# Other PSUM banks for the products of a fused qkv stage, and one place per chunk for its small products

## The reference, cut to what matters

```python
q = _heads(hx, w[:, :hd], na_q_g[j])          # product, then RMS norm over each head's 64 columns
k = _heads(hx, w[:, hd:2 * hd], na_k_g[j])
v = _heads(hx, w[:, 2 * hd:])
k_c = _heads(hc, w[:, hd:2 * hd], na_k_g[j])  # the same for 256 context tokens
v_c = _heads(hc, w[:, 2 * hd:])
x = x + gx1 * (_neighbourhood_attention(q, k, v, k_c, v_c, na_rpb[j]) @ na_w_out[j])
```

## Time and profile before

| | us |
|---|---|
| median of 3 runs | 1366.85 (1366.1 to 1367.48) |
| the profiled execution's own time | 1367.44 |
| its span in the trace | 1365.2 |
| TensorE busy in the span | 1330.2 |
| VectorE, ScalarE, GpSimd busy | 810.3, 594.2, 429.6 |

### The profile page before, as it was taken

The page is one execution under the profiler, slowest core; times in us unless marked ns, Lnnn a source line. Parts: engine busy times, 40 slices in busy tenths (PEclk is TensorE's granted clock), DMA queues, the critical chain, the costliest instruction groups (busy, mean ns, idle before and its releaser), DMA issues.

```text
span 1365.2 us, 20841 instructions
## 1 busy us (share of the span) xinstructions
PE 1330.2 (97%) x8320; PEld 1141.9 (84%) x8320; DVE 810.3 (59%) x1223; ACT 594.2 (44%) x952; POOL 429.6 (31%) x439
## 2 busy tenths in 40 slices
PE   6999999999999999989999999999899999999999
PEld 6888898899997788858878888887577777999999
DVE  6678576899776452386633444343667765855443
ACT  4336545566664132244421244222545544666432
POOL 3443221222420003244400044111466552388200
PEclk9999999999999999999999999999999999999999
DMA  6777457865556231344534444444523221555552
GB/s 256 261 252 270 139 175 275 296 204 184 181 172 207 69 96 59 97 166 156 168 127 156 150 139 146 142 144 159 181 93 108 94 93 32 188 184 185 184 185 78
DMA packets 63967, 220.13 MB, mean 161 GB/s; under 512 B 6912, under 2 KB 10240, under 8 KB 63872
## 3 DMA queue, kind: packets, MB, share of 16 engines
q1 hardware_dynamic: 63584, 218.56, 47.9%
q10 hardware_dynamic: 288, 0.25, 0.1%
HBM read 217.73 MB, written 1.05 MB: 160 GB/s over the span
## 4 chain that ended last, share of the span: by engine, by line
PE 89%; DVE 6%; issue 2%; POOL 1%; ACT 1%; DMA 1%; DVEq 0%; ACTq 0%; POOLq 0%
PE ps L508 26%; PE ps L522 25%; PE ps L520 25%; PE ps L563 2%; PE ps L882 1%; DVE wlo L1463 1%; PE ps L909 1%; PE ps L896 1%; PE ps L828 1%; DVE Alo L1886 1%; DVE tmp L1901 1%; PE ps L875 1%; POOL ssum_c L2094 1%; DVE tmp L1728 1%; PE ps L807 0%
## 5 line engine op out<-in xcount | busy, mean ns | idle before, releaser
L508 PE MATMUL ps<-Ahi,whi 128*128 128x256 f32 (+2 forms) x1640 | 541.4, 330 | 8.3 <-ACT Ahi L1025 5.5
L522 PE MATMUL ps<-Ahi,wlo 128*128 128x256 f32 (+2 forms) x1596 | 510.2, 320 | 0.7 <-DVE wlo L1463 0.6
L520 PE MATMUL ps<-Alo,whi 128*128 128x256 f32 (+2 forms) x1596 | 509.8, 319 | 0.0
L1463 DVE TENSOR_TENSOR wlo<-raw,whi 128x1024 fp32r<-128x1024 f32 x305 | 388.2, 1277 | 104.0 <-ACT whi L1000 104.0
L1000 ACT ACTIVATE whi<-raw 128x1024 fp32r<-128x1024 f32 x305 | 320.1, 1051 | 284.4 <-PE ps L522 220.3
L508 PEld LDWEIGHTS ps<-Ahi,whi 128*128 128x128 f32 x1640 | 312.6, 191 | 73.4 <-issue 30.8
L522 PEld LDWEIGHTS ps<-Ahi,wlo 128*128 128x128 f32 x1596 | 304.5, 191 | 22.7 <-DVE wlo L1463 1.6
L520 PEld LDWEIGHTS ps<-Alo,whi 128*128 128x128 f32 x1596 | 304.5, 191 | 22.4 <-issue 1.7
L520 PE MATMUL ps<-Hlo,whi 128*128 128x256 f32 (+1 forms) x728 | 233.8, 321 | 0.0
L508 PE MATMUL ps<-Hhi,whi 128*128 128x256 f32 (+1 forms) x688 | 222.5, 323 | 0.0
L522 PE MATMUL ps<-Hhi,wlo 128*128 128x256 f32 (+1 forms) x688 | 221.9, 322 | 0.0
(11 more groups left out here) (263 smaller groups left out, 1286.0 us busy)
## 6 DMA issues: line engine op xcount, KB each, us to landing
raw<-in_ada SPq DMA_DIRECT2D x96, 512.0 KB, 4.3
raw<-in_w SPq DMA_DIRECT2D x64, 512.0 KB, 3.5
raw<-in_w_up SPq DMA_DIRECT2D x44, 512.0 KB, 3.9
raw<-in_w_in SPq DMA_DIRECT2D x38, 512.0 KB, 5.1
raw<-in_w_0a SPq DMA_DIRECT2D x32, 512.0 KB, 3.6
raw<-in_w_0b SPq DMA_DIRECT2D x32, 512.0 KB, 3.5
raw<-in_na_in SPq DMA_DIRECT2D x24, 512.0 KB, 5.6
raw<-in_w_down SPq DMA_DIRECT2D x22, 512.0 KB, 3.5
```

The source lines that it names most:

```text
L508: e.matmul(o, w_hi, ah, start=k == 0, stop=False)
L520: e.matmul(o, w_hi, al, start=False, stop=False)
L522: m = e.matmul(o, w_lo, ah, start=False, stop=last)
L1463: e.tensor_tensor(wlo[i % NRAW][:, :cols], raw[i % NRAW][:, :cols], plain(whi[s % NHI][:, :cols]), SUB).then_inc(S("wlo").sem, 1)
```

## The change

`na_in`'s chunks use banks 0 and 1 alternately; every other product keeps its turn among 0, 1 and 2, and `FORMER` names the chunk that last used a chunk's bank. Head sums use bank 2 alone, and each waits until the one before it has been read (a new semaphore `hn_mean`, raised by the mean, also waited for by the first `na_out` chunks). Scores use bank 4 for one head and bank 5 for the other; each waits until the scores two before it in their own count, those of the same head side, have been read.

The head sum or v transposes of chunk n - 1 move from behind the last product of chunk n to the `midway` place of chunk n, behind the step's attention products. That place stays after the fourth of eight steps in a 512-wide chunk. In a 256-wide one (q) it moves behind the eighth step. The sums of the conditioning vectors (`mod_summed`) and their transposes (`written`) stay behind the last product. The orders on VectorE, ScalarE and GpSimd do not change.

```diff
+BANK, FORMER = {}, {}
+for g, key in enumerate(CHUNKS):
+    BANK[key] = key[1] % 2 if key[0] == "na_in" else g % 3
+    FORMER[key] = next((k for k in reversed(CHUNKS[:g]) if BANK[k] == BANK[key]), None)
...
-                if g >= 3:
-                    signal, count = bank_left(*CHUNKS[g - 3])
+                o = ps[BANK[name, n]][:, :Tn]
+                if FORMER[name, n]:
+                    signal, count = bank_left(*FORMER[name, n])
...
-                    if midway and k == kt // 2 - 1:
+                    if midway and k == (kt // 2 if Tn == 512 else kt) - 1:
                         midway(n)
...
+        def head_sum(j, src, T, n):
+            w.wait_ge(S("na"), n + 1)
+            if j:
+                w.wait_ge(S("hn_mean"), j)
             else:
                 w.wait_ge(S("na_t"), 16)
-            return ps[4 + b % 2]
+            e.matmul(ps[2][:, :T], const("blocks"), src, start=True, stop=True).then_inc(S("hn_sum").sem, 1)
...
         def scores2(p, b):
             w.wait_ge(S("hn_out"), 2 * p + 2)
             for x in range(2):
-                o = turn_bank("scores", 4 * p + 2 * b + x)
+                j = 4 * p + 2 * b + x
+                if j >= 2:
+                    w.wait_ge(S("na_bank"), j - 1)
...
+        def midway_na(n):
+            after_na(n - 1)
+            made_na(n - 1)
...
         def out_part(n, pairs):
...
+            w.wait_ge(S("hn_mean"), 16)
...
             if u == 23:
-                during_na(24)
+                made_na(23)
```

More of the change, by code:

```diff
@@ L417, in norm2 @@
         return (2 * c, k2[c % 3], 512) if kind == "k" else (2 * c + 1, q2[c % 3], 256)
[L420 to L427, removed]
     def sync_program(e):
@@ L760, in tensor_program @@
         for n in range(4):
-            g = CHUNK_AT["pool_w", n]
-            o = ps[g % 3][:, :256]
-            signal, count = bank_left(*CHUNKS[g - 3])
+            o = ps[BANK["pool_w", n]][:, :256]
+            signal, count = bank_left(*FORMER["pool_w", n])
             w.wait_ge(S(signal), count)
@@ L880, in scores2 @@
             for x in range(2):
-                o = turn_bank("scores", 4 * p + 2 * b + x)
-                e.matmul(o, q2[p % 3][rows_of(x), 128 * b:128 * b + 128], k2[p % 3][rows_of(x), :],
+                j = 4 * p + 2 * b + x
+                if j >= 2:
+                    w.wait_ge(S("na_bank"), j - 1)
+                else:
+                    w.wait_ge(S("na_t"), 16)
+                e.matmul(ps[4 + x], q2[p % 3][rows_of(x), 128 * b:128 * b + 128], k2[p % 3][rows_of(x), :],
                          start=True, stop=True).then_inc(S("s2_mm").sem, 1)
@@ L911, in product2, with made_na @@
             m.then_inc(S("pv2").sem, 1)
-        def during_na(n):
[L914 to L925, removed]
+        def made_na(m):
+            if norm2(m):
+                j, _, T = norm2(m)
+                head_sum(j, sq[j % 2][:, :T], T, m)
+            elif m >= 0:
+                w.wait_ge(S("na"), m + 1)
+                free6()
+                for t4 in range(4):
+                    t = e.transpose(ps[6][:, 128 * t4:128 * t4 + 128], tmp[4][:, 128 * t4:128 * t4 + 128], ident)
+                t.then_inc(S("v2_tr").sem, 1)
+                bank6[0] = ("v2", NA_CHUNKS[m][1] + 1)
+        def during_na(n):
             mod_summed("na_in", n)
@@ L936, in after_na @@
                 scores2(*scores)
+        def midway_na(n):
+            after_na(n - 1)
+            made_na(n - 1)
         linear("na_in", lambda n: 256 if NA_CHUNKS[n][0] == "q" else 512, lambda k: (Ahi[:, k], Alo[:, k]), ready("na_hi", 2),
-               ready_low("na_lo", "na_lp", 2), during=during_na, midway=lambda n: after_na(n - 1))
+               ready_low("na_lo", "na_lp", 2), during=during_na, midway=midway_na)
         def out_part(n, pairs):
-            g, s = CHUNK_AT["na_out", n], SPLIT_AT["na_out", n]
-            o = ps[g % 3][:, :256]
-            signal, count = bank_left(*CHUNKS[g - 3])
+            s = SPLIT_AT["na_out", n]
+            o = ps[BANK["na_out", n]][:, :256]
+            signal, count = bank_left(*FORMER["na_out", n])
             w.wait_ge(S(signal), count)
+            w.wait_ge(S("hn_mean"), 16)
             w.wait_ge(S("whi"), s + 1)
@@ L1007, in product @@
             w.wait_ge(S("mm"), CHUNK_DONE[name, n])
-            return ps[CHUNK_AT[name, n] % 3]
+            return ps[BANK[name, n]]
         def early_hi(st, into, c, cols, gain):
@@ L1342, in head_root @@
             m, r = tmp[j % 2][:, :T], tmp[2 + j % 2][:, :T]
-            w.wait_ge(S("na_bank"), turn2["norm", j] + 1)
+            w.wait_ge(S("hn_mean"), j + 1)
             if j >= 2:
@@ L1956, in head_mean @@
                 w.wait_ge(S("hn_rr"), j - 1)
-            bank = ps[4 + turn2["norm", j] % 2]
-            e.tensor_scalar(tmp[j % 2][:, :T], bank[:, :T], 1.0 / 64, EPS, MUL, ADD).then_inc(S("na_bank").sem, 1)
+            e.tensor_scalar(tmp[j % 2][:, :T], ps[2][:, :T], 1.0 / 64, EPS, MUL, ADD).then_inc(S("hn_mean").sem, 1)
         def head_out(j, T, dst, gain):
@@ L1980, in scores2 @@
                     w.wait_ge(S("p2_y"), j - 1)
-                turn = turn2["scores", j]
-                bank = ps[4 + turn % 2]
+                bank = ps[4 + x]
                 e.scalar_tensor_tensor(X[x][:, 0:256], bank[:, 0:256], 0.125, bt[h % 4][:, b], MUL, ADD).then_inc(S("na_bias").sem, 1)
                 e.tensor_scalar(X[x][:, 256:512], bank[:, 256:512], 0.125, None, MUL, ALU.bypass).then_inc(S("na_bank").sem, 1)
-                w.wait_ge(S("na_bank"), turn + 1)
+                w.wait_ge(S("na_bank"), j + 1)
                 e.tensor_reduce(m, X[x], AX, MAXOP, negate=True).then_inc(S("s2_max").sem, 1)
```

3 lines of the change are left out of this document (removed).

## The result

The changed kernel takes 1375.28 us (median of 4 runs, 1374.58 to 1378.48); the kernel before, beside it, 1366.47 (4 runs, 1364.81 to 1367.48). The ratio is 1.0070, with a 95% interval of 1.0058 to 1.0082: slower, by 8.8 us. The direction is the forecast one, the time 2.6 us above the 1372.7 forecast. The profiled execution is the slowest of the four, 1378.48 us with a span of 1376.3.

What follows compares the result with a forecast made beforehand. TensorE, busy 1330.2 of 1365.2 us, was taken as the bound. New waits of 12.8 us less 7.0 us removed make it 5.8 us longer, forecast 1372.7 us, range 1365.5 to 1377.5.

Steps and rivals of the forecast that it cites:

- What the change takes away: TensorE in the stage: six bank waits of scores and two waits for the copy of v go, 7.0 us.
- What it costs at nothing: Two banks for chunks and one for head sums add no wait, as the queues' order hides the reads.
- What the move costs: New TensorE waits from chunk 2 to 23, mostly head sums needing `na` earlier than it is raised: 12.8 us.
- From chunk 16 on ... little is lost: Late chunks: old means already followed head sums that keep their place; waits only 0.6, 0.6, 0.65 in 19, 22, 23.
- the replay: All 24 chunks worked through with prices from the trace; `na` of a q comes 9.5 us after its scores start.
- The clock: Rival: one or two clock falls behind new waits in chunks 7, 10, 12, 15; 1374.4 to 1376.1 us, chance 0.22.
- the old fall at 1160: Kernel before, 1160 to 1166 us: granted clock partly at the 1.2 GHz level, costing 1.7 us.
- Unmoved engines: Rival: VectorE, ScalarE and GpSimd keep their old times; new waits 5.7 us, sum -1.3, 1365.6 us, chance 0.15.
- Faster: Rival: the head sum's operand is in time everywhere, all 7.0 us kept; 1359.9 us, chance 0.11.

Runs made afterwards that it cites:

- e1: The kernel before with only the new banks, head sums, v transposes and attention at their old places: 1364.17 us against 1366.10 before, ratio 0.9982.
- e11: The changed kernel with ScalarE doing chunk n's copy and square before the root of chunk n - 1: 1365.82 us, ratio 1.0001 to the kernel before.
- e12: The kernel before with new banks, old places, conditioning transposes behind chunk 4, and ScalarE's copy and square before the root: 1359.13 us against 1366.50.
- e5: The changed kernel itself, measured again with nothing altered: 1374.92 us, ratio 1.0063 to the kernel before.
- e6: The changed kernel with 9, 7, 8 and 7 unused products in TensorE's waits of chunks 7, 10, 12 and 15: 1374.88 us, ratio 1.0063 to before.

## Why the prediction was right, and where its size was off

**What the change takes away, 7.0 us: held.** The waits of scores and for v are gone in the changed kernel. With the banks alone (e1) the two waits for v stay, 1.9 of the 7.0 us, and 2.2 us, by starts, turn into waits for squares. 7.0 - 1.9 - 2.2 = 2.9, and the stage shrank by 2.8.

**What it costs at nothing: held.** No wait for a chunk's bank or for `hn_mean` is in the lists of e1 or of the changed kernel. The reason given was that the copy stands behind the mean anyway. It was the right one: e11 puts the copy ahead of the mean, and the bank wait appears, 2.5 us. It needs the new places too; e12 has the same order on ScalarE with the old places, and no such wait.

**What the move costs, 12.8 us: mechanism right, term too small by 1.8.** The five waits of head sums for squares, chunk by chunk:

| chunk | forecast | wait in the profiled execution |
|---|---|---|
| 6 | 1.0 | 1.11 |
| 7 | 2.8 | 2.57 |
| 10 | 1.65 | 1.84 |
| 12 | 1.8 | 1.71 |
| 15 | 1.7 | 1.84 |

Together 8.95 and 9.07. All new waits by the spacing of starts, from e5 and e6 where no fall blurs them, come to about 14.6 us: chunk 11 (0.3) and 16 (0.55) cost something where I had nothing, 6, 10, 15, 19 and 22 cost 0.2 more each, 7, 13 and 23 a little over 0.1, and chunk 3 cost 1.0, not 1.45. 14.6 - 7.0 = 7.6, against a stage 7.3 us longer. The forecast's "From chunk 16 on ... little is lost" is where the replay was too coarse: chunks 16, 19, 22 and 23 make about 1.05 of the missing 1.8 us.

**The clock: the rival came true in part.** The forecast and this rival were set against each other, and both happened. The new waits of chunks 7, 10, 12 and 15 were the places named, and each had its fall in the profiled execution, two of them in the next one. A fall cost the stage 1.2 us, not 1.7, as part of it is absorbed by later waits. And the old fall at 1160 went. The rest of the median, 8.8 - 7.3 = 1.5 us, is about the size of the clock's difference over whole executions (1.4 to 3.0); that it is the clock is not shown. The measured 1375.28 lies inside this rival's 1374.4 to 1376.1 and 2.6 us from my own time. That agreement is in part luck: of the 3 us between 5.8 and 8.8, half is the term that was too small, and only the other half can be the clock. The stage was to be 5 to 6 us longer; it is 7.3 without falls.

**Unmoved engines: wrong**, as the mean in chunk 7 moved from 1010.28 to 1011.58. **Faster: wrong**: it needed the square within 5.7 us of the scores, and it came at 9.5.

## What to carry to other kernels

Before a consumer is moved earlier, ask when its operand is raised, and follow that back through the in-order queues of the other engines; here one square stood behind a root, a mean and two heads' scores, 9.5 us, and moving two things by half a chunk cost the stage 10.1 us, or 7.3 after what the banks gave back. On the engine that empties PSUM, put the copy that frees TensorE ahead of work that waits for a third engine: that alone was worth 9 us in the changed kernel (6.5 of them in the stage, without clock falls) and 2.4 in the best one. And a bank that costs nothing today may be the next wait once another queue is mended.

## What the runs showed of the hardware

In the changed kernel the granted clock fell to 0.50, the 1.2 GHz level, behind waits of 1.7 to 2.6 us that followed small products, but not in every execution: four times in the stage in one, twice in another, where a wait of 1.84 us in chunk 10 left it full. At that level a 512-wide product takes 0.63 us where it otherwise takes 0.39 to 0.40. The number of falls is part of the scatter between runs. Filling these waits with products kept the granted clock at 1.00 there, but in one execution a fall of 8 us came 17 us behind the stage, and in one of the two kernels with dummies the median showed no gain. A median of a few runs does not price one fall.
